# Moving two samples' cached values from TensorE to VectorE and ScalarE in a hybrid decoder layer

## The chip, the core and the metric

One core of one Trainium2 chip runs the whole layer as one program. The metric is device time in microseconds (us); lower is better. Time before: median 2462.08 us of 3 runs (2461.53 to 2462.41).

## What is computed

One layer of a decoder for a prompt of 512 positions and 8 samples of one token each, 520 columns in all, D_MODEL 2048. A pre-norm and one input projection give q, k, v for 8 stick-breaking attention heads of 128 and u, v for 8 channel groups of a gated MLP. Both outputs are normalised and go through one output projection, then follow a SwiGLU FFN (5632 wide) and an input-embedding gate. The samples attend to 1024 cached positions each, read through a page table: 8 pages of 128 positions. What the change touches is the last line for the samples:

```python
k_past = cache_k[i][page_table]   # (8 samples, 1024, 8 heads, 128), v_past alike
after = lax.cumsum(log_keep, axis=3, reverse=True) - log_keep
a = jnp.where(causal, jnp.exp(jax.nn.log_sigmoid(z) + after), 0.0)
return jnp.einsum('bhqk,bkhd->bqhd', a, v)      # sum over keys of weight x value
```

All is float32; projections are made of three float32r products (high x high, low x high, high x low).

## The kernel before

Activations lie feature-major: 128 partitions of features by 520 columns. The mixer is a sequence of 56 units (`u`), each one weight unit of 16 blocks of 128x128, six products of 260 columns per block. Units 0 to 7 make q, 8 to 23 the MLP's halves, 24 to 39 (from U_KV = 24) k and v in turn, 40 to 47 (U_OUT) the output projection's half fed by the MLP (o_cm), 48 to 55 (U_OUT_SB) its half fed by attention. From unit 40 a unit makes two output tiles, T_OUT + 0 to 31. After unit 55 come the FFN and the gate.

Every engine runs its own list in program order, and waits on semaphores:

- **TensorE** (lines 2067 to 2129) makes the blocks of unit u. Small products are slotted ahead of a block through `between`: in odd units from 25 `sum_later` at block 2, `sum_head` at 6, `attend` at 12, and `scores` after the unit; in even units a transposition at 8. `weigh_values` (line 2036) does a page of cached values: 8 products with a 128x128 stationary block of values and one moving column of weights, put at blocks 7, 11 and 14. Eight pages of a sample take three units from V_FIRST[b] on; samples 6 and 7 (counted from 0) are at units 34 to 36 and 38 to 40. A page's sums lie in spare columns of the unit's PSUM tile. Before a tile, TensorE waits until the tile two back is read (`out_read`, line 1944).
- **VectorE** (line 1500 on) starts its unit u when unit u-1 has ended: `take_values(u-1)`, the take of the tile (`take`, or `out_tile` from u = 41: take times cm_r or sb_r, then add into h), `low_w(u+1)`, then in even units to 38 `keep_head` (which waits for `soft_done`), in odd ones `exponents`, `mask_weights`, `normalise`. `low_x` (line 1359) makes a low part of x. From unit 40 a second `out_tile(2*(u-40))` ends the unit; tiles 0, 6 and 12 first wait for h_in.
- **ScalarE** (line 1020 on) makes w_hi of unit u+1 (`split_w`, when unit u-1 has ended), the logits, exponentials and roots, copies attention out of PSUM, and splits x_hi.
- **POOL** (line 759 on) works through jobs sorted by a due time written as a unit number: page loads into three slots (v_ring's two, acc), each waiting for the page three before to be used; squares of each MLP group and each attention head (512 columns) summed into cm_r and sb_r; and at last, after the last `v_read`, the squares of the 8 sample columns of each head into sb_r, 16 small operations (lines 823 to 826), which signal `sb_sum_done`.
- **SP** (line 655 on) issues loads and stores in the order of its loop over u. Two of h's loads matter here:

```python
                if u == U_OUT + 4:

                    sp.wait_ge(av_ready, HEADS)
                    sp.wait_ge(sb_sum_done, 1)
                    sp.dma_start(h[:, H_PAGES:KT, :], x_t[:, H_PAGES:KT, :]).then_inc(h_in[2], 16)
```

This one (tiles 12 to 15) is line 689; line 684 loads tiles 6 to 11. At the head of its turn u, SP issues the weight load of unit u+3, once unit u+1's low part is done. The sum of sb_r over partitions, its root (ScalarE) and its reciprocal (VectorE) are made in unit SB_ROOT = 45, and x's attention half is split into high and low in units 45, 46 and 47 (3, 3 and 2 heads).

Of the kernel before, what the change touches and what calls it, by code (L numbers as in the profile page):

```python
# [203 lines left out]
CONSTS = 11  # L204
RING = 2
CM_ROOT = U_OUT - 2
SB_ROOT = U_OUT + 5

SB_SPLITS = {U_OUT_SB - 3 + i: range(3 * i, min(3 * i + 3, HEADS)) for i in range(3)}
K_PERIOD = 10  # L210
K_WIDE = K_PER[0] * (U_KV - K_PERIOD)
N_PAGES = SAMPLES * PAGES
# [9 lines left out]


SUM_END = [p + 1 + (p + 1) % 2 for p in LAST_K]
V_FIRST = [16, 19, 22, 25, 28, 31, 34, 38]
V_SLOTS = 3


def v_unit(j):

    b, pg = divmod(j, PAGES)
    return V_FIRST[b] + pg // 3


def v_pages(u):

    return [j for j in range(SAMPLES * PAGES) if v_unit(j) == u]


V_UNITS = [u for u in range(V_FIRST[0], V_FIRST[-1] + 3) if v_pages(u)]  # L240


DIAG = lambda kb: slice(kb * P, (kb + 1) * P)
# [24 lines left out]
def build(nc, w_units, x_t, p_t, cache_k, cache_v, page_table, g_mix, g_out, g_ffn, g_ple, g_q, g_k,  # L268
# [6 lines left out]
    with ExitStack() as ctx:  # L275
# [136 lines left out]

        def v_slot(j):

            return acc[:, :] if j % V_SLOTS == RING else v_ring[:, j % V_SLOTS, :]

        def o_s_ps(u):

            return out_ps[:, 2 * ((tiles_before(u + 1) - 1) % 2) + 1, HALF:HALF + HEADS]

        def raw_slot(slot):

# [63 lines left out]
        consts_in = sem("consts_in")  # L486
        table_in = sem("table_in")
        k_in = [sem(f"k_in{i}") for i in range(3)]
        v_in = [sem(f"v_in{i}") for i in range(V_SLOTS)]
        q_rows_out = sem("q_rows_out")  # L490
        q_rows_in = sem("q_rows_in")
        h_in = [sem(f"h_in{i}") for i in range(3)]
# [71 lines left out]
        ones_built = sem("ones_built")  # L564
        pool_step = sem("pool_step")
        v_used = sem("v_used")
        v_read = sem("v_read")
        h_sum_done = sem("h_sum_done")
        cm_sum_done = sem("cm_sum_done")
# [34 lines left out]
        def _(sp):  # L604
# [50 lines left out]
            for u in range(U_FFN):  # L655
                if u < U_FFN - 1:
                    load_unit(u + 3)
                if u == K_PERIOD - 1:

                    sp.wait_ge(pair_read, 1)  # L660
                    sp.dma_start(q_rows_dram, acc[0:SAMPLES, :]).then_inc(q_rows_out, 16)
                    sp.wait_ge(q_rows_out, 16)

                while u >= K_PERIOD - 1 and next_k < N_PAGES and \
                        (k_before(next_k) is None or k_period(k_before(next_k)) <= u):
                    load_k(next_k)
                    next_k += 1
                if U_KV + 2 <= u <= U_OUT and u % 2 == 0:
                    i = (u - U_KV - 2) // 2
                    sp.wait_ge(norm_done, 2 * HEADS + i + 1)  # L670
                    sp.dma_start(k_t[i], k_head[:, :]).then_inc(k_out, 16)
                    sp.wait_ge(out_read, U_KV + 2 * i + 2)
                    sp.dma_start(v_t[i], y[:, 1, :]).then_inc(v_out, 16)
                if u == U_KV + 2:
                    sp.wait_ge(cm_done, HEADS)
                    sp.dma_start(chunk_v_t, chunk_v[:, :, :]).then_inc(chunk_out, 16)
                if u == LAST_K[-1] + 3:

                    sp.wait_ge(z_s_done, SAMPLES)
                    sp.dma_start(h[:, 0:H_KEYS, :], x_t[:, 0:H_KEYS, :]).then_inc(h_in[0], 16)  # L680
                if u == V_UNITS[-1] + 2:

                    sp.wait_ge(v_used, N_PAGES)
                    sp.dma_start(h[:, H_KEYS:H_PAGES, :], x_t[:, H_KEYS:H_PAGES, :]).then_inc(h_in[1], 16)
                if u == U_OUT + 4:

# [72 lines left out]
        def _(pool):  # L759
# [25 lines left out]

            def load_v(j):
                page = pool.value_load(table[0:1, j:j + 1], min_val=0, max_val=N_PHYS - 1)
                if j >= V_SLOTS:
                    pool.wait_ge(v_used, j - V_SLOTS + 1)
                elif j % V_SLOTS == RING:  # L790
                    pool.wait_ge(q_rows_out, 16)
                pool.dma_start(v_slot(j),
                               cache_v[bass.ds(page, 1), :, :].rearrange("a p n -> (a p) n"))\
                    .then_inc(v_in[j % V_SLOTS], 16)

            def add_squares(x, total, cols, done=pool_step):
                chained(pool.tensor_tensor(pool_sq[:, cols], x, x, ALU.mult))
# [5 lines left out]
                    pool.wait_ge(done, 1)  # L803


            jobs = [(v_unit(j - V_SLOTS) + 0.8, "load", j) for j in range(V_SLOTS, N_PAGES)]
            jobs += [(U_MLP + 3.5 + 2 * i, "mlp", i) for i in range(HEADS)]
            jobs += [(U_KV + 3.7 + 2 * i, "attention", i) for i in range(HEADS)]
            pool.wait_ge(table_in, 16)
            pool.wait_ge(x_lo_done, KT)  # L810
            pool.wait_ge(sq_done, X_SQUARES)
# [73 lines left out]
        def _(act):  # L885
# [76 lines left out]
            def weights_of_sample(u):  # L962

                if u - 1 in SUM_END:
# [3 lines left out]
                        act.wait_ge(v_used, PAGES * (b - 2))  # L968
                    act.activation(a_s[:, b % 3, :], z_s[:, :], ACT.Exp).then_inc(a_s_done, 1)

            def sample_job(u):

                if u not in SUM_END:
                    return []
                act.wait_ge(z_s_done, SUM_END.index(u) + 1)
                return [(soft_s[:, :], z_s[:, :], soft_s_done)]
# [43 lines left out]
            for u in range(1, U_FFN):  # L1020
# [35 lines left out]
                elif u < U_OUT and u % 2 == 1:  # L1056
# [8 lines left out]
                    rstd(2 * HEADS + i)  # L1065
                    if not i:
                        weights_of_sample(u)
                    if i:
                        take_attention(i - 1)
                elif u <= U_OUT:  # L1070
# [38 lines left out]
                if u == SB_ROOT:  # L1109
                    root(2, HEADS * P, sb_r[:, :])  # L1110
                    load_ln_exp()
                if u in SB_SPLITS:
                    for k in SB_SPLITS[u]:
                        split(x_hi[:, k, :], q[:, k, :], gain_out[:, k:k + 1])
# [226 lines left out]
        def _(dve):  # L1341
# [72 lines left out]

            def take_values(u):

                if u not in V_UNITS:
                    return
                b = v_pages(u)[0] // PAGES
                dve.wait_ge(out_done, tiles_before(u + 1))  # L1420
                sums = q[:, :, PROMPT + b]
                if u == V_FIRST[b]:
                    dve.tensor_copy(sums, o_s_ps(u)).then_inc(v_read, 1)
                else:
                    dve.wait_ge(v_read, V_UNITS.index(u))
                    dve.tensor_tensor(sums, sums, o_s_ps(u), ALU.add).then_inc(v_read, 1)

            def weigh_sample(b):
                dve.wait_ge(later_s_ready, b + 1)
# [70 lines left out]
            for u in range(1, U_FFN):  # L1500
# [63 lines left out]
                elif u <= U_OUT and u % 2 == 0:  # L1564
# [5 lines left out]
                    low_w(u + 1, 1)  # L1570
                    score_next()
                    if u < U_OUT:
                        keep_head(i)
                    if u in SUM_END:
                        keep_sample(SUM_END.index(u))
# [9 lines left out]
                if U_KV < u < U_OUT and u % 2 == 1:  # L1585
# [10 lines left out]
                    if i:  # L1596
                        dve.wait_ge(k_out, 16 * i)
                    normalise(2 * HEADS + i, k_head[:, :], y[:, t % 2, :], gain_k[:, 0:1])
                if u == CM_ROOT:
                    invert(1, cm_r[:, :])  # L1600
                if u == SB_ROOT:
                    invert(2, sb_r[:, :])
# [4 lines left out]
                    keep_sample(SUM_END.index(u))  # L1607
                while pages:
                    score_next()
                if u == U_OUT_SB + 2:  # L1610
                    for k in range(2):
                        dve.wait_ge(p_hi_done, k + 1)
                        dve.tensor_tensor(p_lo[:, k, :], p_raw[:, k, :], p_hi[:, k, :], ALU.subtract)\
                            .then_inc(p_lo_done, 1)
# [303 lines left out]
        def _(pe):  # L1918
# [117 lines left out]
            def weigh_values(j, u):  # L2036
# [5 lines left out]
                pe.wait_ge(v_in[j % V_SLOTS], 16 * (j // V_SLOTS + 1))  # L2042
                if j == pages[0] and V_UNITS.index(u) > 1:
                    pe.wait_ge(v_read, V_UNITS.index(u) - 1)
                for hd in range(HEADS):
                    at = pg * HEADS + hd
                    mm = pe.matmul(o_s_ps(u)[:, hd:hd + 1], v_slot(j)[:, hd * P:(hd + 1) * P],  # L2047
                                   a_s[:, b % 3, at:at + 1], start=False, stop=j == pages[-1],
                                   skip_group_check=True)
                mm.then_inc(v_used, 1)  # L2050

            def sum_later_sample(b, u):
                pe.wait_ge(keep_s_done, b + 1)
# [13 lines left out]
            for u in range(1, U_FFN):  # L2067
# [30 lines left out]

                for at, j in zip((14, 11, 7), reversed(v_pages(u))):
                    between[at] = lambda j=j, u=u: weigh_values(j, u)  # L2100
                if u - 1 in SUM_END:
                    between[4] = lambda u=u: sum_later_sample(SUM_END.index(u - 1), u - 1)

# [286 lines left out]
```

## Time and profile before

| | us |
|---|---|
| median of 3 runs | 2462.08 |
| profiled execution | 2461.91 |
| its span | 2460.3 |
| TensorE busy in the span | 2428.4 |
| VectorE busy | 1724.0 |
| ScalarE busy | 1118.4 |
| POOL busy | 374.2 |

The granted TensorE clock was 0.999 of 2.4 GHz. The mixer's units 34 to 48 lie from 566.7 to 794 us; stretches are named by the time at which VectorE begins its turn, which is when TensorE has ended the projection of the unit before. A row of a stretch is: its ends, its length, busy us (x instructions) of TensorE, its weight loads, VectorE, ScalarE and POOL, then the granted clock, the DMA engines' busy share and GB/s. A row in order of time is: start us, duration us, engine, line, operation. "x2" behind an entry means that two instructions are merged in it; a bracket gives the idle time of the engine before it and what ended that.

### The profile page before, as it was taken

The page shows a single profiled execution, that of the slowest core. Times are in us where ns is not written, and L with a number is a line of the kernel's source. Part 1 is how long each engine was busy: PE and PEld are TensorE (multiplying, and loading weights), DVE is VectorE, ACT ScalarE, POOL GpSimd, SP SyncE. Part 2 cuts the span into 40 slices and gives each one's busy share as a digit, 9 for nine tenths or more (in the row PEclk, how much of TensorE's full clock was granted, in tenths as well). Part 3 has the DMA queues.
Part 4 walks back from the last instruction along what each step waited for, and adds up shares of the span by engine and source line. Part 5 has one row for each costly group of instructions (what it writes and reads, how often), then busy time and mean ns, then how long its engine had stood idle before and what let it go on. Part 6 is the DMA issues. An engine that isn't in the chain of part 4 may idle for free.

```text
span 2460.3 us, 47595 instructions
## 1 busy us (share of the span) xinstructions
PE 2428.4 (99%) x19952; PEld 2405.6 (98%) x19952; DVE 1724.0 (70%) x2172; ACT 1118.4 (45%) x1655; POOL 374.2 (15%) x375
## 2 busy tenths in 40 slices
PE   8999999999999998999999999999999999999999
PEld 7999999999999998999999999999999999999999
DVE  5379767564446478888888888888888888877333
ACT  6333233333433365555555555555555555555221
POOL 0011111111001220121212121111112121223000
PEclk9999999999999999999999999999999999999999
DMA  6256766463423452474757565656566666695323
GB/s 217 94 189 213 249 224 220 164 209 124 160 104 105 146 173 90 123 175 125 169 130 164 134 160 137 163 136 159 141 152 146 148 152 144 155 197 215 122 86 104
DMA packets 135590, 382.61 MB, mean 156 GB/s; under 512 B 14026, under 2 KB 58186, under 8 KB 126674
## 3 DMA queue, kind: packets, MB, share of 16 engines
q1 hardware_dynamic: 72450, 285.16, 33.9%
q0 software_dynamic: 62640, 94.28, 20.2%
q8 instruction: 158, 2.59, 0.4%
q14 instruction: 54, 0.44, 0.1%
q10 hardware_dynamic: 288, 0.14, 0.0%
HBM read 309.18 MB, written 73.55 MB: 156 GB/s over the span
## 4 chain that ended last, share of the span: by engine, by line
PE 86%; DVE 9%; ACT 2%; issue 2%; DMA 1%; SPq 0%; ACTq 0%; DVEq 0%; POOL 0%
PE out_ps L1925 24%; PE tok_mix L2158 15%; PE pair_ps L2158 12%; PE out_ps L2142 9%; PE out_ps L2158 8%; PE out_ps L2047 4%; PE out_ps L2231 4%; PE pair_ps L2231 2%; DVE w_sum L1637 2%; DVE w_lo L1625 2%; PE pair_ps L1964 1%; PE tok_mix L2231 1%; DVE w_lo L1630 1%; ACT w_hi L1134 1%; DVE staging L1786 1%
## 5 line engine op out<-in xcount | busy, mean ns | idle before, releaser
L1925 PE MATMUL out_ps<-x_hi,w_hi 128*128 128x260 f32 x1792 | 378.6, 292 | 10.1 <-DVE w_lo L1480 8.3
L1134 ACT ACTIVATE w_hi<-w_sum 128x1024 fp32r<-128x1024 f32 (+1 forms) x252 | 215.4, 855 | 343.1 <-DVE w_sum L1637 247.9
L1925 PE MATMUL out_ps<-x_hi,w_lo 128*128 128x260 f32 x1792 | 361.1, 283 | 0.0
L1925 PE MATMUL out_ps<-x_lo,w_hi 128*128 128x260 f32 x1792 | 360.8, 283 | 0.0
L1625 DVE TENSOR_TENSOR w_lo<-w_sum,w_hi 128x1024 fp32r<-128x1024 f32 (+1 forms) x252 | 244.7, 971 | 135.0 <-ACT w_hi L1134 134.5
L1134 ACT ACTIVATE w_hi<-w_raw 128x1024 fp32r<-128x1024 f32 (+1 forms) x306 | 261.2, 865 | 133.7 <-PE out_ps L2142 102.4
L2158 PE MATMUL tok_mix<-op_hi,w_hi 128*128 128x260 f32 x1056 | 297.3, 282 | 2.1 <-ACT part L1176 1.9
L2158 PE MATMUL tok_mix<-op_hi,w_lo 128*128 128x260 f32 x1056 | 298.1, 282 | 0.0
L2158 PE MATMUL tok_mix<-op_lo,w_hi 128*128 128x260 f32 x1056 | 297.5, 282 | 0.0
L1925 PEld LDWEIGHTS out_ps<-x_hi,w_hi 128*128 128x128 f32 x1792 | 278.5, 189 | 12.7 <-DVE w_lo L1480 8.3
L854 POOL DMA_DIRECT2D h_dram<-staging x110 | 146.9, 1489 | 926.7 <-DVE staging L1786 909.4
L1925 PEld LDWEIGHTS out_ps<-x_hi,w_lo 128*128 128x128 f32 x1792 | 276.5, 189 | 0.0
L1925 PEld LDWEIGHTS out_ps<-x_lo,w_hi 128*128 128x128 f32 x1792 | 276.5, 189 | 0.0
L2158 PE MATMUL pair_ps<-op_hi,w_hi 128*128 128x260 f32 x880 | 248.5, 282 | 9.1 <-DVE op_lo L1828 5.0
L2158 PE MATMUL pair_ps<-op_hi,w_lo 128*128 128x260 f32 x880 | 248.9, 283 | 0.0
L2158 PE MATMUL pair_ps<-op_lo,w_hi 128*128 128x260 f32 x880 | 248.5, 282 | 0.0
L1625 DVE TENSOR_TENSOR w_lo<-w_raw,w_hi 128x1024 fp32r<-128x1024 f32 x172 | 209.5, 1222 | 44.7 <-ACT w_hi L1134 44.7
L898 ACT ACTIVATE w_hi<-w_raw 128x1024 fp32r<-128x1024 f32 x114 | 114.3, 1050 | 210.8 <-PE out_ps L1925 210.6
L2158 PEld LDWEIGHTS tok_mix<-op_hi,w_hi 128*128 128x128 f32 x1056 | 198.2, 188 | 2.6 <-ACT part L1176 2.1
L2158 PEld LDWEIGHTS tok_mix<-op_hi,w_lo 128*128 128x128 f32 x1056 | 198.5, 188 | 0.0
L2158 PEld LDWEIGHTS tok_mix<-op_lo,w_hi 128*128 128x128 f32 x1056 | 198.2, 188 | 0.0
L2158 PEld LDWEIGHTS pair_ps<-op_hi,w_hi 128*128 128x128 f32 x880 | 165.8, 188 | 10.0 <-issue 8.3
(291 smaller groups left out, 6106.3 us busy)
## 6 DMA issues: line engine op xcount, KB each, us to landing
w_raw<-w_units SPq DMA_DIRECT2D x239, 512.0 KB, 4.1
w_raw<-w_units SPq DMA_DIRECT2D x57, 1024.0 KB, 5.0
w_fifth<-w_units SPq DMA_DIRECT2D x58, 512.0 KB, 3.8
h_dram<-staging POOLq DMA_DIRECT2D x110, 260.0 KB, 7.0
k_ring<-cache_k SPq DMA_DIRECT2D x50, 512.0 KB, 5.2
v_ring<-cache_v POOLq DMA_DIRECT2D x43, 512.0 KB, 4.7
h_dram<-part POOLq DMA_DIRECT2D x50, 260.0 KB, 6.6
acc<-cache_v POOLq DMA_DIRECT2D x21, 512.0 KB, 5.2
```

Of the source, the lines that this page charges most:

```text
L854: pool.dma_start(dst, stage(k), accum_op=op).then_inc(h_added[DOWN_SLOT[k]], 16)
L898: act.activation(w_hi[:, u % 2, cols], w_raw[:, u % 2, cols], ACT.Copy).then_inc(hi_done, 1)
L1134: act.activation(dst, src, ACT.Copy).then_inc(hi_done, 1)
L1625: dve.tensor_tensor(slot(w_lo, job), src, slot(w_hi, job), ALU.subtract).then_inc(lo_done, 1)
L1630: dve.tensor_tensor(as_blocks(slot(w_lo, job)), src, as_blocks(slot(w_hi, job)), ALU.subtract)\
L1637: dve.tensor_tensor(dst, x, w, op).then_inc(w_summed, 1)
L1786: dve.tensor_tensor(stage(k), stage(k), (bank_y, bank_v)[n], ALU.add).then_inc(sums_staged, 1)
L1925: mm = pe.matmul(out_ps[:, 2 * (t % 2) + a, 0:HALF], w[:, u % 2, cols], x[:, a * HALF:(a + 1) * HALF], start=first and n == 0, stop=last a ...
L2047: mm = pe.matmul(o_s_ps(u)[:, hd:hd + 1], v_slot(j)[:, hd * P:(hd + 1) * P], a_s[:, b % 3, at:at + 1], start=False, stop=j == pages[-1], s ...
L2142: mm = pe.matmul(tile[:, a, :], w, x[:, a * HALF:(a + 1) * HALF], start=first and n == 0, stop=last and n == 2)
L2158: mm = pe.matmul(acc, w, x[:, g, :], start=fresh and g == 0 and n == 0, stop=g == GROUPS - 1 and n == 2, skip_group_check=True)
L2231: mm = pe.matmul(DOWN_BANKS[i][:, a, :], w, x, start=fresh and c == 0 and n == 0, stop=c == 1 and n == 2, skip_group_check=True)
```

## The change

Samples 0 to 5 stay as they are. Sample 6 (pages 48 to 55): VectorE multiplies each page in place by its weights, broadcast along the 128 values of a head, and adds the pages to one total, two pages a unit in units 35 to 38. Sample 7 (pages 56 to 63): ScalarE scales each head's 128 columns of a page by its weight, 8 instructions a page, in units 39 and 41 to 44; VectorE adds the pages in units 40 and 42 to 45. A total is summed over partitions by TensorE with 8 products against one column of ones (`sum_total`), at block 14 of units 39 and 45. Four more slots for pages and a total are cut out of o_cm, once its low parts are made. SB_ROOT moves from unit 45 to 47, the splits of attention to units 46 and 47 (5 and 3 heads), cm_r's reciprocal from unit 38 to 39, POOL's job for the last head to 43.9, and h's load of tiles 6 to 11 from SP's turn 42 to 40. SP's load at turn 44 keeps its place and its waits. V_UNITS becomes a list of pairs (unit, sample) and ends with 45, so that the last `v_read` comes at the start of VectorE's turn 46.

```diff
 CM_ROOT = U_OUT - 2
-SB_ROOT = U_OUT + 5
-
-SB_SPLITS = {U_OUT_SB - 3 + i: range(3 * i, min(3 * i + 3, HEADS)) for i in range(3)}
+SB_ROOT = U_OUT + 7
+
+SB_SPLITS = {U_OUT_SB - 2: range(0, 5), U_OUT_SB - 1: range(5, HEADS)}
...
-V_FIRST = [16, 19, 22, 25, 28, 31, 34, 38]
+V_FIRST = [16, 19, 22, 25, 28, 31]
 V_SLOTS = 3
+O_SLOTS = 4
+BY_TENSOR = len(V_FIRST)
+N_TENSOR = BY_TENSOR * PAGES
+SIXTH, SEVENTH = N_TENSOR, N_TENSOR + PAGES
+
+
+WEIGH_UNIT = dict(zip(range(SIXTH, N_PAGES), (35, 35, 36, 36, 37, 37, 38, 38) + (39, 39, 41, 41, 42, 43, 43, 44)))
+ADD_UNIT = dict(zip(range(SIXTH, N_PAGES), (35, 35, 36, 36, 37, 37, 38, 38) + (40, 40, 42, 42, 43, 44, 44, 45)))
+V_REDUCE = {39: BY_TENSOR, 45: BY_TENSOR + 1}
+V_SLOT = [j % V_SLOTS for j in range(SIXTH + 1)] + [1 + n % 2 for n in range(PAGES - 1)] + [2, 1, 4, 5, 6, 4, 5, 6]
+V_TOTAL = {BY_TENSOR: V_SLOT[SIXTH], BY_TENSOR + 1: V_SLOTS}
...
+def v_freed(j):
+
+    return v_unit(j) if j < N_TENSOR else ADD_UNIT[j]
...
+def v_before(j):
+
+    return max((i for i in range(j) if V_SLOT[i] == V_SLOT[j]), default=None)
...
+        def v_place(i):
+
+            if i >= V_SLOTS:
+                first = (i - V_SLOTS) * HEADS * P
+                return o_cm[:, :, :].rearrange("p h n -> p (h n)")[:, first:first + HEADS * P]
+            return acc[:, :] if i == RING else v_ring[:, i, :]
...
@@ block.sync
-                if u == V_UNITS[-1] + 2:
-
-                    sp.wait_ge(v_used, N_PAGES)
+                if u == U_OUT:
+
+                    sp.wait_ge(v_used, N_TENSOR)
+                    sp.wait_ge(total_used, 1)
+                    sp.wait_ge(v_added, added(SEVENTH + 1))
                     sp.dma_start(h[:, H_KEYS:H_PAGES, :], x_t[:, H_KEYS:H_PAGES, :]).then_inc(h_in[1], 16)
                 if u == U_OUT + 4:
 
...
@@ block.gpsimd
-                if j >= V_SLOTS:
-                    pool.wait_ge(v_used, j - V_SLOTS + 1)
-                elif j % V_SLOTS == RING:
+                before = v_before(j)
+                if before is None and V_SLOT[j] >= V_SLOTS:
+                    pool.wait_ge(x_lo_done, KT + HEADS)
+                elif before is not None and before < N_TENSOR:
+                    pool.wait_ge(v_used, before + 1)
+                elif before is not None:
+                    pool.wait_ge(v_added, added(before))
+                elif V_SLOT[j] == RING:
                     pool.wait_ge(q_rows_out, 16)
...
-            jobs = [(v_unit(j - V_SLOTS) + 0.8, "load", j) for j in range(V_SLOTS, N_PAGES)]
+            freed = [U_OUT - 0.3 if v_before(j) is None else v_freed(v_before(j)) for j in range(V_SLOTS, N_PAGES)]
+            jobs = [(freed[j - V_SLOTS] + 0.8, "load", j) for j in range(V_SLOTS, N_PAGES)]
             jobs += [(U_MLP + 3.5 + 2 * i, "mlp", i) for i in range(HEADS)]
-            jobs += [(U_KV + 3.7 + 2 * i, "attention", i) for i in range(HEADS)]
+            jobs += [(U_KV + 3.7 + 2 * i, "attention", i) for i in range(HEADS - 1)]
+            jobs += [(U_OUT + 3.9, "attention", HEADS - 1)]
...
@@ block.scalar
+            def weigh_page(j):
+
+                b, pg = divmod(j, PAGES)
+                act.wait_ge(a_s_done, b + 1)
+                act.wait_ge(v_in[V_SLOT[j]], 16 * (v_turn(j) + 1))
+                for hd in range(HEADS):
+                    values = v_slot(j)[:, hd * P:(hd + 1) * P]
+                    at = pg * HEADS + hd
+                    ins = act.activation(values, values, ACT.Copy, scale=a_s[:, b % 3, at:at + 1])
+                ins.then_inc(v_scaled, 1)
...
                     if not i:
                         weights_of_sample(u)
+                    weigh_pages(u)
                     if i:
                         take_attention(i - 1)
...
                     take_attention(HEADS - 1)
+                if u > U_OUT:
+                    weigh_pages(u)
...
+                if u == min(SB_SPLITS):
+                    act.wait_ge(v_read, len(V_UNITS))
                 if u in SB_SPLITS:
...
@@ block.vector
+            def weigh_page(j):
+
+                b, pg = divmod(j, PAGES)
+                dve.wait_ge(v_in[V_SLOT[j]], 16 * (v_turn(j) + 1))
+                values = v_slot(j).rearrange("p (h d) -> p h d", h=HEADS)
+                weights = a_s[:, b % 3, pg * HEADS:(pg + 1) * HEADS].unsqueeze(2).to_broadcast([P, HEADS, P])
+                if pg == 0:
+                    dve.wait_ge(a_s_done, b + 1)
+                chained(dve.tensor_tensor(values, values, weights, ALU.mult), v_weighed)
+
+            def add_page(j):
+
+                b, pg = divmod(j, PAGES)
+                if b > BY_TENSOR:
+                    dve.wait_ge(v_scaled, pg + 1)
+                if j == SEVENTH + 1:
+                    dve.wait_ge(x_lo_done, KT + HEADS)
+                total = v_place(V_TOTAL[b])
+                chained(dve.tensor_tensor(total, v_slot(j - 1) if pg == 1 else total, v_slot(j), ALU.add), v_added)
+
+            def pages_of(u):
+
+                for j in range(SIXTH, N_PAGES):
+                    if j < SEVENTH and WEIGH_UNIT[j] == u:
+                        weigh_page(j)
+                    if ADD_UNIT[j] == u and j % PAGES:
+                        add_page(j)
...
                     score_next()
                     if u < U_OUT:
+                        pages_of(u)
                         keep_head(i)
...
-                if u == CM_ROOT:
+                if u == CM_ROOT + 1:
                     invert(1, cm_r[:, :])
...
                 while pages:
                     score_next()
+                if u % 2 or u >= U_OUT:
+                    pages_of(u)
...
@@ block.tensor
+            def sum_total(u, b):
+
+                pe.wait_ge(v_added, added(PAGES * b + PAGES - 1))
+                pe.wait_ge(v_read, V_UNITS.index((u, b)))
+                total = v_place(V_TOTAL[b])
+                for hd in range(HEADS):
+                    mm = pe.matmul(o_s_ps(u, b)[:, hd:hd + 1], total[:, hd * P:(hd + 1) * P], ones[:, 0:1],
+                                   start=False, stop=True, skip_group_check=True)
+                mm.then_inc(total_used, 1)
...
                 for at, j in zip((14, 11, 7), reversed(v_pages(u))):
                     between[at] = lambda j=j, u=u: weigh_values(j, u)
+                if u in V_REDUCE:
+                    between[14] = lambda u=u: sum_total(u, V_REDUCE[u])
```

## Rows read from the trace of the kernel before

**Rows 1.** The page: the span, and the first line of its busy times.

```profile
span 2460.3 us, 47595 instructions
...
PE 2428.4 (99%) x19952; PEld 2405.6 (98%) x19952; DVE 1724.0 (70%) x2172; ACT 1118.4 (45%) x1655; POOL 374.2 (15%) x375
```

**Rows 2.** The chain of waits, unit 36: start us, us, what.

```profile
617.98 2.15 PE out_ps L1925 x18
620.13 1.68 PE out_ps L2047 x16
621.81 2.27 PE out_ps L1925 x18
```

**Rows 3.** Stretches: units 37 to 39, 42, 43, 45 (columns: see above).

```profile
627.40:645.90 18.50, 18.50 (x139) 17.06 (x138) 6.61 (x10) 5.88 (x8) 2.17 (x2) 1.00 0.47 172
645.90:666.30 20.40, 20.40 (x169) 19.97 (x168) 11.05 (x11) 11.40 (x12) 1.80 (x4) 1.00 0.42 131
666.30:689.60 23.30, 23.30 (x182) 21.86 (x181) 6.20 (x8) 5.72 (x8) 2.71 (x3) 1.00 0.21 68
...
718.80:736.00 17.20, 17.20 (x130) 15.89 (x129) 7.41 (x9) 3.28 (x3) 0.00 (x0) 1.00 0.40 155
736.00:747.50 11.50, 11.50 (x98) 11.50 (x97) 6.03 (x6) 2.49 (x3) 6.72 (x18) 1.00 0.28 93
...
759.10:771.50 12.40, 12.40 (x103) 12.28 (x102) 10.58 (x10) 7.24 (x8) 0.00 (x0) 1.00 0.26 86
```

**Rows 4.** VectorE's groups by form, 560 to 830 us: key product.

```profile
L1385 DVE TENSOR_TENSOR k_ring<-k_ring,q_rows 128x1024 f32<-128x1024 f32 x2 | 2.4, 1223 | 0.0
```

**Rows 5.** VectorE in order of time, unit 38.

```profile
647.07 2.36 DVE L1354 TENSOR_TENSOR w_lo<-w_raw,w_hi 128x1024 fp32r<-128x1024 f32 x2 [0.42 <-ACT w_hi L898]
653.71 1.49 DVE L1444 SCALAR_TENSOR_TENSOR keep<-z,soft 128x1280 f32<-128x1280 f32 x1 [4.27 <-ACT soft L960]
```

**Rows 6.** POOL in order of time, units 35 and 37; v_ring's landings.

```profile
609.26 0.59 POOL L792 DMA_DIRECT2D v_ring<-cache_v  x1 [1.22 <-issue]
...
644.77 1.28 POOL L798 TENSOR_TENSOR sb_r<-sb_r,pool_sq 128x512 f32<-128x512 f32 x1
...
DMA to landing us min/median/max: 3.4/3.7/5.1
```

**Rows 7.** ScalarE: two forms (busy us, mean ns), one instruction of unit 39.

```profile
L946 ACT ACTIVATE v_tok<-tok_mix 128x512 f32<-128x512 f32 x14 | 8.3, 596 | 39.5 <-PE tok_mix L1976 39.5
...
L969 ACT ACTIVATE a_s<-z_s 128x64 f32<-128x64 f32 x8 | 2.0, 251 | 16.9 <-DVE dot_pad L1434 16.9
...
684.92 0.60 ACT L951 ACTIVATE q<-tok_mix 128x512 f32<-128x512 f32 x1 [8.69 <-PE tok_mix L2032]
```

**Rows 8.** POOL, then VectorE, in order of time, unit 43.

```profile
739.73 2.15 POOL L798 TENSOR_TENSOR sb_r<-sb_r,pool_sq 128x512 f32<-128x512 f32 x1
741.96 0.20 POOL L797 TENSOR_TENSOR pool_sq<-q 128x8 f32<-128x8 f32 x1
...
742.80 0.54 POOL L798 TENSOR_TENSOR sb_r<-sb_r,pool_sq 128x8 f32<-128x8 f32 x1
...
746.47 0.20 POOL L798 TENSOR_TENSOR sb_r<-sb_r,pool_sq 128x8 f32<-128x8 f32 x1
...
737.52 3.21 DVE L1354 TENSOR_TENSOR w_lo<-w_raw,w_hi 128x1024 fp32r<-128x1024 f32 x2
...
742.55 0.72 DVE L1471 TENSOR_TENSOR h<-h,sq 128x520 f32<-128x520 f32 x1
```

**Rows 9.** VectorE in order of time, unit 45.

```profile
763.15 3.40 DVE L1368 RECIPROCAL sb_r<-sb_r 128x520 f32<-128x520 f32 x1 [0.20 <-ACT sb_r L914]
766.59 2.10 DVE L1363 SCALAR_TENSOR_TENSOR x_lo<-q,gain_out,x_hi 128x520 fp32r<-128x520 f32 x3
```

**Rows 10.** Line 689, h's tiles 12 to 15 (1040 KB): landing.

```profile
DMA to landing us min/median/max: 6.7/6.7/6.7
```

**Rows 11.** Line 610, weights of 1024 KB, 560 to 830 us: landing.

```profile
DMA to landing us min/median/max: 4.6/5.0/8.4
```

More of the change, by code:

```diff
@@ L224, with v_pages, v_turn, added @@
 SUM_END = [p + 1 + (p + 1) % 2 for p in LAST_K]
-V_FIRST = [16, 19, 22, 25, 28, 31, 34, 38]
+V_FIRST = [16, 19, 22, 25, 28, 31]
 V_SLOTS = 3
-def v_unit(j):
+O_SLOTS = 4
[7 more added lines that the diff above has]
+V_TOTAL = {BY_TENSOR: V_SLOT[SIXTH], BY_TENSOR + 1: V_SLOTS}
+def v_unit(j):
+    return V_FIRST[j // PAGES] + j % PAGES // 3
+def v_pages(u):
+    return [j for j in range(N_TENSOR) if v_unit(j) == u]
+def v_freed(j):
+    return v_unit(j) if j < N_TENSOR else ADD_UNIT[j]
+def v_turn(j):
+    return V_SLOT[:j].count(V_SLOT[j])
+def v_before(j):
+    return max((i for i in range(j) if V_SLOT[i] == V_SLOT[j]), default=None)
+def added(j):
     b, pg = divmod(j, PAGES)
[L232 to L240, printed above, removed]
+    return (PAGES - 1) * (b - BY_TENSOR) + pg
+V_UNITS = sorted([(u, b) for b in range(BY_TENSOR) for u in range(V_FIRST[b], V_FIRST[b] + 3)] + list(V_REDUCE.items()))
 DIAG = lambda kb: slice(kb * P, (kb + 1) * P)
@@ L413, in v_slot, with o_s_ps @@
         def v_slot(j):
-            return acc[:, :] if j % V_SLOTS == RING else v_ring[:, j % V_SLOTS, :]
-        def o_s_ps(u):
-            return out_ps[:, 2 * ((tiles_before(u + 1) - 1) % 2) + 1, HALF:HALF + HEADS]
+            return v_place(V_SLOT[j])
+        def v_place(i):
[3 more added lines that the diff above has]
+            return acc[:, :] if i == RING else v_ring[:, i, :]
+        def o_s_ps(u, b):
+            first = HALF + HEADS * (b % 2)
+            return out_ps[:, 2 * ((tiles_before(u + 1) - 1) % 2) + 1, first:first + HEADS]
         def raw_slot(slot):
@@ L488, in build @@
         k_in = [sem(f"k_in{i}") for i in range(3)]
-        v_in = [sem(f"v_in{i}") for i in range(V_SLOTS)]
+        v_in = [sem(f"v_in{i}") for i in range(V_SLOTS + O_SLOTS)]
         q_rows_out = sem("q_rows_out")
@@ L566, in build @@
         v_used = sem("v_used")
+        v_weighed = sem("v_weighed")
+        v_added = sem("v_added")
+        total_used = sem("total_used")
+        v_scaled = sem("v_scaled")
         v_read = sem("v_read")
@@ L793, in load_v @@
                                cache_v[bass.ds(page, 1), :, :].rearrange("a p n -> (a p) n"))\
-                    .then_inc(v_in[j % V_SLOTS], 16)
+                    .then_inc(v_in[V_SLOT[j]], 16)
             def add_squares(x, total, cols, done=pool_step):
@@ L969, in weights_of_sample, with weigh_pages @@
                     act.activation(a_s[:, b % 3, :], z_s[:, :], ACT.Exp).then_inc(a_s_done, 1)
+            def weigh_page(j):
[7 more added lines that the diff above has]
+                ins.then_inc(v_scaled, 1)
+            def weigh_pages(u):
+                for j in range(SEVENTH, N_PAGES):
+                    if WEIGH_UNIT[j] == u:
+                        weigh_page(j)
             def sample_job(u):
@@ L1415, in take_values @@
             def take_values(u):
[L1417 to L1426, printed above, removed]
+                for n, (v_u, b) in enumerate(V_UNITS):
+                    if v_u == u:
+                        dve.wait_ge(out_done, tiles_before(u + 1))
+                        sums = q[:, :, PROMPT + b]
+                        if b >= BY_TENSOR or u == V_FIRST[b]:
+                            dve.tensor_copy(sums, o_s_ps(u, b)).then_inc(v_read, 1)
+                        else:
+                            dve.wait_ge(v_read, n)
+                            dve.tensor_tensor(sums, sums, o_s_ps(u, b), ALU.add).then_inc(v_read, 1)
+            def weigh_page(j):
[17 more added lines that the diff above has]
+                    if j < SEVENTH and WEIGH_UNIT[j] == u:
+                        weigh_page(j)
+                    if ADD_UNIT[j] == u and j % PAGES:
+                        add_page(j)
             def weigh_sample(b):
@@ L2041, in weigh_values @@
                     pe.wait_ge(a_s_done, b + 1)
-                pe.wait_ge(v_in[j % V_SLOTS], 16 * (j // V_SLOTS + 1))
-                if j == pages[0] and V_UNITS.index(u) > 1:
-                    pe.wait_ge(v_read, V_UNITS.index(u) - 1)
+                pe.wait_ge(v_in[V_SLOT[j]], 16 * (v_turn(j) + 1))
+                n = V_UNITS.index((u, b))
+                if j == pages[0] and n > 1:
+                    pe.wait_ge(v_read, n - 1)
                 for hd in range(HEADS):
                     at = pg * HEADS + hd
-                    mm = pe.matmul(o_s_ps(u)[:, hd:hd + 1], v_slot(j)[:, hd * P:(hd + 1) * P],
+                    mm = pe.matmul(o_s_ps(u, b)[:, hd:hd + 1], v_slot(j)[:, hd * P:(hd + 1) * P],
                                    a_s[:, b % 3, at:at + 1], start=False, stop=j == pages[-1],
```

## The prediction

> **What bounds the kernel now.** I read the page first: of a span of 2460.3 us TensorE is busy 2428.4, and every other engine far less [rows 1]. So any work that leaves TensorE shortens the run, as long as nothing makes TensorE wait instead. The profiled execution took 2461.91 us (1.6 around its span), 0.17 below the median of the three runs, 2462.08; I make the sum against 2461.91 and add the 0.17 back. A measurement of this kernel can tell about 0.2%, 4.9 us, from no change.
>
> Second, the chain of work through the mixer. It is all TensorE, without a gap, and says what a page of values costs there: a piece of 1.68 us for its 8 products (two records each) [rows 2]. The 18 records of projection behind a page take 2.27 us where the 18 ahead of it take 2.15, so the page also costs 0.12 at its seam. I take 1.79 (other seams show 0.11); bounds are 1.68 and, for seams at both ends, 1.85.
>
> Third, the stretches by unit [rows 3]. In units 38 and 39 TensorE is busy throughout, VectorE 11.05 of 20.4 us and 6.20 of 23.3, ScalarE 11.40 and 5.72. There is room for the moved work by its sum. What must be checked is its place in each queue.
>
> **TensorE's part.** Sixteen pages leave, at units 34, 35, 36 and 38, 39, 40; two totals of 8 products against a column of ones come, at 39 and 45. They have the form of a page, so I price them as one. Net 14 x 1.79 = 25.1 us saved (bounds 23.5 and 25.9). It comes off fully if nothing below is late.
>
> **VectorE in units 35 to 38.** It gets 8 products and 7 sums of 128x1024. The nearest row is the key product of the same shape, 1.22 us [rows 4]; with its wait 1.25. Even units put four of them, 5.0 us, between low_w and keep_head. In unit 38 (start 645.9) low_w ends 3.5 us in, and keep_head, which waits for ScalarE's soft, starts 7.8 us in [rows 5]. So 4.3 us were idle and page work fills them. One gate is ahead: pages 54 and 55 are loaded by POOL behind its squares of head 5, which end at 646.05, 0.1 us into the unit; the load follows 1.2 us later [rows 6] and lands in 3.7 us (at most 5.1), 5 to 6.5 us into the unit. Then four operations end at 10.3, and keep_head with its 4.8 us at about 15. The unit itself shrinks from 20.4 to 20.4 - 5.4 = 15.0. Behind the waiting instruction stand keep_head and the next take; TensorE needs keep_head two blocks (1.35 us) into unit 39, at 16.3. Slack 1.3 us: cost zero, and up to 1.5 if the page lands late or goes unhidden. Unit 36 is alike. Its sample bookkeeping stands behind keep_head and is wanted only at block 4. In odd units the page work stands last, where VectorE has done its 6.20 us of 23.3 [rows 3] and waits for the next take. The same holds for the inversion of cm_r, moved from unit 38 to 39: 3.40 us by its twin [rows 9], beside TensorE's work.
>
> **ScalarE.** It gets 64 scalings of 128x128. Bounds are 0.25 us (the 128x64 exponential) and 0.60 (128x512); by the line between them about 0.3 [rows 7]. In unit 39 two pages are 16 of them, some 5 us, where ScalarE had 8.69 us idle ahead of taking the attention, from 10 us into the unit [rows 7]; with two pages gone ahead of it the attention comes 15 us in, so 5 fit. In units 41 to 44 ScalarE is busy 2.5 to 3.3 us of 11.5 to 17.2 [rows 3] and gets at most 5. Cost nothing; uncovered, at 0.6 each, 5 us late, and later units still hide that, because VectorE adds a unit later (the last page: scaled in 44, added in 45, used at block 14 of 45).
>
> **VectorE, units 40 to 45.** Seven sums, at most two a unit (2.5 us), in units like 42 and 43, where it is busy 7.41 of 17.2 and 6.03 of 11.5 [rows 3]. Hidden: its next take of a first half comes no earlier than 5.8 us in, and TensorE needs that only at the next unit's start.
>
> **What moves late: the sb sum.** This is the part with a price. POOL squares the eight samples' columns, 16 small operations, only after the last v_read. That read was at unit 41; it is now at the start of unit 46 (call this T). Three things wait for the result. The sum over partitions, moved to unit 47, is not late. But SP's load of x into h, tiles 12 to 15, still stands at its old place in the loop, unit 44, and waits for sb_sum_done; behind it in SP's queue stands the weight load of unit 48. And VectorE waits for that h in out_tile(12), in unit 46.
>
> POOL's 16 operations took from 741.96 to 746.67, 4.7 us [rows 8]. There VectorE was mostly idle. Where it was not, they blocked each other: POOL's sum at 742.80 took 0.54 in place of 0.20 beside VectorE's h sum (742.55, 0.72), POOL's 128x512 sum took 2.15 beside low_w, and the two low_w 3.21 in place of 2.36. In unit 46 POOL starts with VectorE's busiest stretch: one h sum (0.70), two low_w (2.36) and five x_lo (0.70 each, from 2.10 for three [rows 9]), all reading two SBUF tensors, 6.5 us together. With every one of the eight holding POOL once, less POOL's gap of 0.08 each: 0.3 + 4.7 + 6.5 - 0.6 = 10.8 us after T. Bounds: 5.0 (no hold) and 11.4.
>
> The Trainium skill ("SBUF — State Buffer", section Who interferes with whom) says that a VectorE instruction with two SBUF inputs and a GpSimd one that reads SBUF fully block each other, the first to issue holding the port; by that rule the sum is ready near 10.8, without it near 5.0. The trace agrees, with the 0.54 and the 2.15 above.
>
> Then SP issues (0.1), the load lands in 6.7 us (its own row [rows 10]; at least 5 by a weight load of the same size [rows 11]), and the take adds 0.75: T + 18.3. TensorE reaches the end of unit 46 at T + 11.5 [rows 3] and its next tile needs exactly that take. **Wait: 6.8 us**; bounds 0 (5.0 + 0.1 + 5.0 + 0.75 = 10.9, before 11.5) and about 8.5.
>
> Next in line is unit 48. Its weights, issued at T + 11.3 behind the h load, land in at most 8.4 us (T + 19.7) [rows 11]; ScalarE splits them, then root and reciprocal (3.40), three x_lo and the take of tile 14 follow, which I put at T + 30.2, against TensorE's T + 18.3 + 12.4 [rows 3] = 30.7. Nothing, or up to 2 us.
>
> SP's other h load moves from 42 to 40 and waits for page 57's sum, some 10 us into unit 40; the weight load ahead of it is out by then and the next is due in unit 41, so nothing queues up. It and the page loads share DMA engines that the rows show 0.21 to 0.47 busy [rows 3].
>
> **Sum.** -25.1 + 6.8 = -18.3; 2461.91 - 18.3 + 0.17 = 2443.8 us. Past unit 56 all is gated by TensorE's own progress and carries the shift unchanged.
>
> **Rivals.**
> 1. *POOL is not held up, or the load is quick* (0.22). For: small operations may slip in between VectorE's. Against: the 0.54 row. Wait 0 to 2: 2437 to 2439.
> 2. *Forecast* (0.58): wait 4 to 8.5, 2441 to 2446.
> 3. *More than one place is late* (0.12): keep_head misses unit 39 by 1.5, the take of tile 14 misses unit 48 by 2, page scalings hold split_w once by 2: 2443.8 + 5.5, so 2447 to 2456. For: slacks of 1.3 and 0.4 us. Against: all rest on measured rows.
> 4. *Slower* (0.05), one mechanism: VectorE stands at v_in ahead of keep_head in units 36 and 38, because POOL loads those pages behind its squares. Each us beyond the slack of 1.3 is a us of TensorE, twice. To lose 18.3 and a measurable 5 more, each load must be 13 us late, landing in 17 us where the rows show 3.7, at most 5.1: about 2467.
> The remaining 0.03 is for gains and losses that meet within 0.2%. That the change doesn't do what it says I exclude: pages 48 to 63 leave TensorE by the loop's own bound.
>
> **Range.** 2436.5 (first rival, full saving) to 2448.5: it takes in rival 1, the forecast and the start of 3. Faster by over 0.2%: 0.92; within 0.2%: 0.03; slower: 0.05.
>
> **What would show it.** TensorE's page products down from 1024 records to 768, plus 32 for totals; units 35, 36, 38 at 18.0, 14.1, 15.0 us. One wait of TensorE near the start of unit 47, on VectorE's take, of about 7 us, itself behind DMA of h. POOL's 16 small operations stretched to some 10 us. If TensorE waits in 39, rival 3 or 4; if nowhere, rival 1 and 25 us saved. I am wrong if the saving per page is not near 1.8, or if the wait stands elsewhere.

## The result, and the profile after

The changed kernel took 2445.25 us (median of 4 runs, 2443.67 to 2446.13) against 2462.24 for the kernel before on the same chip: a ratio of 0.993, 95% interval 0.9913 to 0.9948. The forecast was 2443.8. (One of e_wfirst's four executions below took 6080.08 us; its median is of the other three.) The profiled execution's span went from 2460.3 to 2443.6 us, 16.7 less. The number is close; two of its terms were off in opposite directions, and a third was missing, as the rows below show.

The page of the changed kernel, with the first lines of its busy times and of its chain (compare rows 1):

```profile
span 2443.6 us, 47247 instructions
...
PE 2409.5 (99%) x19728; PEld 2386.2 (98%) x19728; DVE 1749.0 (72%) x2190; ACT 1137.6 (47%) x1719; POOL 377.9 (15%) x375
...
PE 84%; DVE 9%; ACT 2%; issue 2%; DMA 1%; POOL 0%; SPq 0%; ACTq 0%; DVEq 0%; POOLq 0%
```

TensorE has 224 records less (112 products of two) and VectorE 25.0 us more work. TensorE's share of the chain went from 86% to 84%. The stretches of the changed kernel, for units 36, 38, 39, 45, 46, 47 and 48 (columns as in rows 3):

```profile
599.00:613.10 14.10, 14.10 (x116) 13.78 (x115) 13.14 (x17) 8.75 (x11) 1.85 (x4) 1.00 0.69 225
...
631.60:646.60 15.00, 15.00 (x120) 14.57 (x120) 9.33 (x8) 11.38 (x11) 2.43 (x5) 1.00 0.66 211
646.60:668.70 22.10, 20.11 (x150) 18.46 (x150) 12.74 (x14) 10.53 (x23) 2.30 (x2) 1.00 0.22 73
...
734.70:747.90 13.20, 13.20 (x114) 13.20 (x113) 6.30 (x7) 2.01 (x2) 0.00 (x0) 1.00 0.00 1
747.90:763.20 15.30, 12.11 (x99) 11.94 (x98) 8.56 (x12) 5.11 (x7) 7.51 (x16) 0.94 0.34 128
763.20:777.90 14.70, 14.70 (x102) 14.30 (x101) 10.61 (x11) 7.24 (x8) 0.00 (x0) 0.83 0.41 155
777.90:789.50 11.60, 11.60 (x99) 11.60 (x98) 5.16 (x6) 2.01 (x2) 0.00 (x0) 1.00 0.39 138
```

Unit 38 went from 20.4 us [rows 3] to 15.0 and unit 36 measures 14.1, both as forecast. Unit 35 measures 16.9, not the forecast 18.0: VectorE, busy until then, began its turn at 582.2, 1.2 us after ScalarE, which waits for the same end of unit 34. Units 34 and 35 together went from 43.0 to 32.3, which is six pages of 1.79. Unit 39 should have taken 23.3 - 3 x 1.79 + 1.79 = 19.7 and took 22.1, with TensorE busy 20.11. Unit 46 took 15.3 in place of 11.5, busy 12.11. Unit 47 took 14.7 in place of 12.4 with TensorE busy throughout, but its granted clock was 0.83, and 0.94 in the stretch before. So three things were paid: about 2.3, 3.7 and 2.4 us. 25.1 - 2.3 - 3.7 - 2.4 = 16.7, the whole difference of the spans.

For TensorE itself the last two divide otherwise, because the bound between units 46 and 47 is VectorE's turn, at 763.27, and TensorE had gone on at 762.65. TensorE stood 3.2 us. Its granted clock fell to half (1.2 GHz) at about 761.5, while it still stood, and rose again at 768.3; these are its first 5.65 us of work behind the wait:

```profile
762.65:768.30 5.65, 5.65 (x22) 5.25 (x23) 4.35 (x5) 3.98 (x5) 0.00 (x0) 0.50 0.60 254
```

So the low clock cost 5.65 / 2 = 2.8 us, and wait and clock together 6.0 of the 6.1.

TensorE's waits, changed kernel, whose longest is over 1.9 us (engine, line, for whom: us in total, times, longest). The first two belong to the start and to the FFN and are about as they were; the third is in unit 47, the fourth in 39:

```profile
PE out_ps L2029 <- DVE w_lo L1581: 7.8, 1, 7.8
PE pair_ps L2275 <- DVE op_lo L1932: 5.0, 1, 5.0
PE out_ps L2029 <- DVE sq L1452: 3.2, 1, 3.2
PE pair_ps L2113 <- DVE soft L1553: 2.0, 1, 2.0
```

**The wait in unit 39.** The chain of waits of the changed kernel through unit 38, pieces left out:

```profile
628.75 0.61 ACT q L1003
...
629.44 1.05 POOL pool_sq L847
...
630.55 1.30 POOL sb_r L848
...
634.22 8.40 DMA v_ring<-cache_v
...
642.71 1.24 DVE v_ring L1509
643.97 1.23 DVE v_ring L1519
645.23 1.50 DVE keep L1545
...
650.01 1.13 PE pair_ps L2113 x2
```

It is the gate that the prediction named: POOL's squares of head 5, then the load of page 55, then VectorE's product and sum, then keep_head, then TensorE's sum_later in unit 39. But the load of page 55 took 8.4 us, where rows 6 show 3.7 and at most 5.1. It was also issued 1.2 us behind that of page 54, which landed in 4.9. VectorE in order of time, unit 38, shows both page waits (compare rows 5, where keep_head starts 7.8 us into the unit; here it is 13.6):

```profile
637.97 1.23 DVE L1509 TENSOR_TENSOR acc<-acc,a_s 128x1024 f32<-128x1024 f32 x1 [2.75 <-DMA acc<-cache_v]
639.23 1.23 DVE L1519 TENSOR_TENSOR v_ring<-v_ring,acc 128x1024 f32<-128x1024 f32 x1
642.71 1.23 DVE L1509 TENSOR_TENSOR v_ring<-v_ring,a_s 128x1024 f32<-128x1024 f32 x1 [2.26 <-DMA v_ring<-cache_v]
```

The product with a broadcast operand costs 1.23 us, as its nearest row did (rows 4: 1.22). ScalarE's 16 scalings of two pages took 4.79 us in units 41 and 43, 0.30 each, as estimated.

**The wait in unit 47.** POOL in order of time, changed kernel, unit 46 (compare rows 8), then VectorE there:

```profile
748.35 0.20 POOL L847 TENSOR_TENSOR pool_sq<-q 128x8 f32<-128x8 f32 x1 [27.77 <-DVE q L1496]
748.64 0.21 POOL L848 TENSOR_TENSOR sb_r<-sb_r,pool_sq 128x8 f32<-128x8 f32 x1
748.92 0.69 POOL L847 TENSOR_TENSOR pool_sq<-q 128x8 f32<-128x8 f32 x1
749.69 1.18 POOL L848 TENSOR_TENSOR sb_r<-sb_r,pool_sq 128x8 f32<-128x8 f32 x1
750.95 1.06 POOL L847 TENSOR_TENSOR pool_sq<-q 128x8 f32<-128x8 f32 x1
752.08 0.59 POOL L848 TENSOR_TENSOR sb_r<-sb_r,pool_sq 128x8 f32<-128x8 f32 x1
...
756.84 0.20 POOL L848 TENSOR_TENSOR sb_r<-sb_r,pool_sq 128x8 f32<-128x8 f32 x1
```

```profile
749.58 2.37 DVE L1428 TENSOR_TENSOR w_lo<-w_raw,w_hi 128x1024 fp32r<-128x1024 f32 x2
751.87 3.43 DVE L1437 SCALAR_TENSOR_TENSOR x_lo<-q,gain_out,x_hi 128x520 fp32r<-128x520 f32 x5
761.80 0.70 DVE L1452 TENSOR_TENSOR sq<-out_ps,cm_r 128x520 f32<-128x520 f32 x1 [6.50 <-DMA h<-x_t]
```

Eight of POOL's sixteen operations are stretched: 0.69, 1.18, 1.06 and five of 0.59. The chain of sixteen lasts 8.7 us, from 748.35 to 757.04, where it was 4.7. SP issues the h load at 757.12 and it lands in 4.7; VectorE's take, 6.5 us idle before it, starts at 761.80, and TensorE goes on at 762.65, having stood 3.19 us.

### The profile page after: what moved, and what is told of

The parts are those of the page before. It is cut to its first block, busy times and chain, and to the rows that moved or that the text cites. A ratio compares the mean times of both kernels' runs of the same rounds, so it can differ in the third digit from the quotient of the medians.

```text
span 2443.6 us, 47247 instructions
## 1 busy us (share of the span) xinstructions
PE 2409.5 (99%) x19728; PEld 2386.2 (98%) x19728; DVE 1749.0 (72%) x2190; ACT 1137.6 (47%) x1719; POOL 377.9 (15%) x375
## 4 chain that ended last, share of the span: by engine, by line
PE 84%; DVE 9%; ACT 2%; issue 2%; DMA 1%; POOL 0%; SPq 0%; ACTq 0%; DVEq 0%; POOLq 0%
PE out_ps L2029 24%; PE tok_mix L2275 15%; PE pair_ps L2275 12%; PE out_ps L2259 9%; PE out_ps L2275 8%; PE out_ps L2348 5%; PE out_ps L2152 3%; PE pair_ps L2348 3%; DVE w_lo L1729 2%; DVE w_sum L1741 2%; PE tok_mix L2348 1%; PE pair_ps L2068 1%; ACT w_hi L1208 1%; DVE w_lo L1734 1%; DMA w_raw<-w_units 1%
```

## The experiments

Each time is a median; the kernel before took 2461.67 beside the first four and 2462.01 beside the last three. The 95% interval of each ratio reaches 0.17%, some 4 us, to either side. So the times alone do not settle differences of 0.5 to 2.5 us between two versions; there the traces carry the argument.

**Only the products leave TensorE (e_price).** An edit of the kernel before, which leaves out seven of the eight heads' sums for samples 6 and 7:

```diff
-                for hd in range(HEADS):
+                for hd in range(HEADS if j < 6 * PAGES else 1):
                     at = pg * HEADS + hd
```

> The kernel before, with 112 products left out and nothing put in their place: of the 16 pages of samples 6 and 7, TensorE makes only the first head's product of the eight (the other heads' sums for these two samples are left out). That is the same net number of products that the change takes from TensorE. Theory (a page costs 1.79 us at every place, and 14 pages' worth are worth 25.1): 2462.1 - 25.1 = 2437.0, no waits of TensorE in units 34 to 48, no lower clock there. Rival (products beside projections are partly hidden, so they are worth less, and the change lost nothing but some of this saving): 2443 to 2446.

Measured: 2436.86 us, ratio 0.9899 (0.9882 to 0.9915), 24.8 us less than the kernel before beside it; TensorE waits nowhere from unit 34 to 48 (busy 240.00 of the 240 us from 560 to 800), and its clock is whole until the FFN. The products are worth 1.77 to 1.79 us a page in full, so the change loses some 8 us elsewhere.

**POOL's order (e_due).** On the changed kernel:

```diff
-            jobs += [(U_KV + 3.7 + 2 * i, "attention", i) for i in range(HEADS - 1)]
+            jobs += [(U_KV + 3.9 + 2 * i, "attention", i) for i in range(HEADS - 1)]
```

> The changed kernel, with POOL's squares of heads 0 to 6 due 0.2 of a unit later, so that they stand behind the page loads of the same unit instead of ahead. Theory (the 2.0 us wait of TensorE in unit 39 comes from pages 54 and 55 landing late, ahead of keep_head in VectorE's queue): both pages land before VectorE comes to them in unit 38, keep_head starts about 8.5 us into the unit instead of 13.5, the wait in unit 39 is gone: 2445.2 - 2.2 = 2443.0; the wait at unit 47 stays. Rival (VectorE simply has too much ahead of keep_head in unit 38, wherever the pages are): the wait stays at 1 to 2 us, 2445.

Measured: 2443.22 us, ratio 0.9921 (0.9904 to 0.9937), 2.0 less than the changed kernel. VectorE in order of time, e_due, unit 38 (start 632.3):

```profile
635.95 1.21 DVE L1509 TENSOR_TENSOR acc<-acc,a_s 128x1024 f32<-128x1024 f32 x1
...
640.98 1.49 DVE L1545 SCALAR_TENSOR_TENSOR keep<-z,soft 128x1280 f32<-128x1280 f32 x1
```

No wait for a page is left, keep_head starts 8.6 us into the unit, and TensorE's wait in unit 39 is gone: the unit takes 19.8 us in place of 22.1. So it was the page's lateness, not the amount of VectorE's work. The wait at unit 47 stays, at 3.3. The low clock behind it is shorter here, about 3.5 us in place of 6.8.

**The h load freed from the sample squares (e_scratch).** On the changed kernel (`squared` is a new semaphore):

```diff
-                    sp.wait_ge(sb_sum_done, 1)
+                    sp.wait_ge(squared, 1)
...
-                    add_squares(q[:, i, 0:PROMPT], sb_r, slice(0, PROMPT))
+                    add_squares(q[:, i, 0:PROMPT], sb_r, slice(0, PROMPT), squared if i == HEADS - 1 else pool_step)
...
-                            sb_sum_done if i == HEADS - 1 else pool_step)
+                            sb_sum_done if i == HEADS - 1 else pool_step, z)
```

> The changed kernel, with the sample squares put in a buffer that h does not cover (the free z), so that SP's load of h, tiles 12 to 15, waits only for the last head's squares in unit 43. Theory (that load is what TensorE waits for at the start of unit 47, and the half-clock stretch of 6.8 us behind it follows from that wait): the wait of 3.2 us and the half-clock stretch are both gone, unit 46 back to 11.5 us and unit 47 to 12.4: 2445.2 - 3.7 - 2.4 = 2439.1. Rival A (sample squares still bound unit 47 through the sum of sb_r): a wait of 1 to 3 us moves into unit 47 or 48. Rival B (the lower clock has nothing to do with the wait): it stays somewhere in units 46 to 48, 2441.5.

Measured: 2439.59 us, ratio 0.9909 (0.9892 to 0.9925), 5.7 less than the changed kernel. The stretches of e_scratch, units 46 and 47:

```profile
748.40:759.95 11.55, 11.55 (x98) 11.55 (x97) 8.51 (x12) 5.11 (x7) 8.00 (x16) 1.00 0.26 92
759.95:772.30 12.35, 12.35 (x102) 12.23 (x101) 10.57 (x10) 7.24 (x8) 0.00 (x0) 1.00 0.23 86
```

Both units are back at 11.55 and 12.35 us, at a whole clock, though POOL's sixteen operations are as slow as before (8.00 us busy). POOL's lateness alone cost nothing; it cost through h's load. The wait in unit 39 is still there, 2.4 us in this trace.

**SP's order (e_wfirst).** On the changed kernel:

```diff
-                if u == U_OUT + 4:
+                if u == U_OUT + 6:
 
                     sp.wait_ge(av_ready, HEADS)
```

> The changed kernel, with SP's load of h, tiles 12 to 15, and its waits moved from turn 44 of SP's loop to turn 46, so that the weight loads of units 48 and 49 stand ahead of it. Theory (the h load alone counts, and it cannot start before the sample squares are summed): nothing changes but ScalarE's wait of 11 us for unit 48's weights, the wait at unit 47 stays at 3 to 4 us: 2445 within 0.7. Rival (the weight load held back in SP's queue counts too): 2 us or more are won.

Measured: 2444.75 us, ratio 0.993 (0.991 to 0.9949): no gain clear of noise, 0.5 less than the changed kernel. ScalarE no longer waits 11 us for unit 48's weights. TensorE's wait is 3.3, and the low clock stands behind it again, for 6.8 us as in the changed kernel. What SP held back behind its wait was not needed sooner.

**Both repairs (e_both).** The edits of e_due and e_scratch together.

> The changed kernel with both repairs: POOL's squares of heads 0 to 6 due behind the page loads (as in e_due), and the sample squares in z, so that h's load waits only for the last head's squares (as in e_scratch). Theory (the two waits are independent and all that was lost besides the clock): all 25.1 us of the removed products come through, no wait of TensorE over 1 us from unit 34 to unit 48 and no half-clock stretch there: 2462.0 - 25.1 = 2437.0. Rival (one repair uncovers something that the other hid, such as VectorE late at unit 48): 2439 or more.

Measured: 2437.98 us (2437.10 to 2438.96), ratio 0.9902 (0.9886 to 0.9919), 24.0 less than the kernel before beside it and 7.3 less than the changed kernel. In e_both TensorE waits nowhere between units 34 and 48:

```profile
560.00:800.00 240.00, 240.00 (x1909) 232.53 (x1908) 157.60 (x182) 112.38 (x174) 34.80 (x45) 1.00 0.41 140
```

It is the best version of the study, and within 1.1 us of e_price, where the products were simply left out.

**VectorE's x_lo out of POOL's way (e_xlo_late).** On the changed kernel:

```diff
-                if u in SB_SPLITS:
+                if u in SB_SPLITS and u > min(SB_SPLITS):
...
                     out_tile(2 * (u - U_OUT), cm_r if u < U_OUT_SB else sb_r)
+                if u == min(SB_SPLITS):
+                    for k in SB_SPLITS[u]:
+                        low_x(k, q[:, k, :], gain_out[:, k:k + 1])
```

> The changed kernel, with VectorE's five x_lo of unit 46 moved from ahead of out_tile(12) to behind it. Theory (POOL's small squares are held up by VectorE's operations with two SBUF inputs, one each): five of POOL's sixteen take 0.20 again in place of 0.59, the chain of sixteen shrinks from 8.7 to 6.8 us, h lands 1.9 us earlier, TensorE's wait at unit 47 falls from 3.2 to 1.3, and the half-clock stretch may go with it: 2443.3, or 2441 without that stretch. Rival (POOL is slow there for another reason, such as its own start or ScalarE's splits, which stay): the chain stays at 8.7 us, 2445.

Measured: 2443.80 us, ratio 0.9924 (0.9908 to 0.9941). POOL in order of time, e_xlo_late, unit 46:

```profile
751.46 1.06 POOL L847 TENSOR_TENSOR pool_sq<-q 128x8 f32<-128x8 f32 x1
752.60 0.20 POOL L848 TENSOR_TENSOR sb_r<-sb_r,pool_sq 128x8 f32<-128x8 f32 x1
...
755.38 0.20 POOL L848 TENSOR_TENSOR sb_r<-sb_r,pool_sq 128x8 f32<-128x8 f32 x1
```

The three operations beside the h sum and low_w stay slow (0.69, 1.18, 1.06); the five that ran beside x_lo take 0.20. The chain is 6.7 us (748.87 to 755.58), and TensorE's wait for the take 1.3. So x_lo, a VectorE operation with two inputs in SBUF, is what held those five; for the h sum and low_w the overlap in time says the same, but they were not moved. The total fell by 1.45 us, less than the wait, though the clock is whole here from 758 to 780 us. The x_lo now make VectorE late in unit 47, and TensorE stands a second time, for 1.3 us. From the start of unit 46 to the second take of unit 48 this trace is 2.9 us shorter than the changed kernel's, so the other 0.9 of its span's 2.0 less was lost again outside these units.

**A wait made by VectorE alone (e_filler).** On e_both:

```diff
+                if u == min(SB_SPLITS):
+                    for _ in range(2):
+                        chained(dve.reciprocal(soft[:, 0:TOK], soft[:, 0:TOK]))
                 if u >= U_OUT:
```

> The kernel e_both with two reciprocals of 128x520 (3.4 us each, on the spare tile soft) put on VectorE ahead of out_tile(12) in unit 46, so that TensorE must wait again at the start of unit 47, this time for no DMA and no POOL. VectorE's x_lo end 7.2 us into unit 46, the take then at 14.1 to 14.8, so the wait is about 3.2 us. Theory (the half-clock stretch follows from TensorE's own idling): a stretch at half clock of 3.4 to 6.8 us stands right behind the wait and costs 1.2 to 2.4 us over it: 2437.0 + 3.2 + 1.2 to 2.4, so 2441.4 to 2442.6. Rival (it came with the late DMA or POOL work): the clock stays whole, 2440.2.

Measured: 2442.25 us (2440.83 to 2443.02), 4.3 over e_both. The profiled execution is the quickest, 2440.83. In it TensorE waits 3.5 us, and the stretch behind the wait (unit 47, with most of that wait in it) has a whole clock:

```profile
757.90:773.00 15.10, 12.12 (x98) 12.03 (x98) 13.99 (x13) 6.85 (x8) 0.00 (x0) 1.00 0.21 71
```

So here the wait was not enough to lower the clock. The other three executions took 1.0 to 2.2 us more, with mean clocks of 0.997, 0.996 and 0.998, which leaves room for such a stretch in some of them; no trace shows where. The expectation is not met in the one place where it was looked for.

That TensorE's idling by VectorE alone can be followed by the low clock is shown elsewhere in the traces, the one before the change included. In the FFN of the kernel before, TensorE stands 4.96 us for VectorE's op_lo with POOL and the DMA engines idle for the first 4.5 us of it, and goes on at 927.31:

```profile
PE pair_ps L2158 <- DVE op_lo L1828: 5.0, 1, 5.0
...
927.31:930.10 2.79, 2.79 (x13) 2.79 (x14) 2.79 (x3) 0.68 (x1) 0.00 (x0) 0.50 0.43 163
```

In e_filler the same wait is followed by 3.1 us at 0.50, and a wait of 2.3 us for VectorE's w_lo, with the DMA engines idle, by 3 us more. So the rival, that the low clock belongs to a late DMA or to POOL's work, falls; that it follows every such wait falls too.

## Why the prediction was right

- **TensorE's part: right.** 14 pages x 1.79 = 25.1. Units 36 and 38 came out at 14.1 and 15.0 as forecast, e_price took off 24.8 and e_both 24.0.
- **VectorE in 35 to 38: the price right, the zero wrong.** Its operations cost what the key product did. The step that failed is "lands in 3.7 us (at most 5.1)": page 55 took 8.4, keep_head ended at 649.95 where TensorE wanted it at about 648.0, and TensorE stood 2.0 us, 2.3 over the unit. The prediction also gave pages 54 and 55 one landing, where the second load was issued 1.2 us behind the first. I had taken the landing from page loads of the kernel before, issued at other points of the unit. That page 55 shared the DMA engines with unit 41's weights and the k and v stores, issued 1.0 to 2.3 us behind it, fits the stretch's DMA share of 0.66 against 0.42 [rows 3], but was not tried apart. (Two weight loads issued right behind h's load, at 757.49, left that one at 4.7.) e_due shows that the order of the load against POOL's squares decides. The prediction gave this as a possible 1.5 us, and as part of its third rival.
- **ScalarE, and VectorE from 40 to 45: right.** No wait of TensorE stands there.
- **The sb sum: right in place and in mechanism, too dear.** Forecast a wait of 6.8 us, measured 3.2. Two terms were mis-sized. POOL was done 9.1 us after T, not 10.8: I added POOL's own 0.20 to each time that it was blocked, but a blocked operation took 0.59 beside an x_lo that repeats every 0.68, so its last part ran beside VectorE's next; and VectorE was not slowed (2.37 for two low_w, 2.36 before), unlike beside POOL's wide operations [rows 8]. And h landed in 4.7, not 6.7: in the kernel before, a weight load was issued 0.1 us ahead of it; here none was. In e_scratch, where one is again issued right ahead, h's load lands in 7.1, and in e_due, e_wfirst and e_xlo_late, without one, in 4.8. With these, 9.1 + 0.1 + 4.7 + 0.8 - 11.5 = 3.2, as measured. Two bounds of the prediction do not come out of its rows: "at least 5" for the landing (rows 11 show 4.6), and "about 8.5" for the wait, where 11.4 + 0.1 + 6.7 + 0.75 - 11.5 makes 7.5. Rival 1 was half right: POOL was held up, and e_xlo_late shows by what for five of eight, but the load was quick. The wait of 3.2 lies between rival 1's 0 to 2 and the forecast's 4 to 8.5, in neither.
- **Unit 48's start: right.** The held weight load cost nothing, and e_wfirst shows it.
- **Missing: the clock.** The prediction had no term for it. 5.65 us of TensorE's work behind the wait ran at 1.2 GHz, which cost 2.8 us.

The three errors are -3.6, +2.3 and +2.8 us. They sum to 1.5, against 1.45 between forecast and median. So the closeness of the total is luck in good part: more than one place was late, as the third rival says, but with a total inside the forecast's 2441 to 2446. The sign is no luck, since all that was lost, 8.4 us, is a third of what the products gave.

## What to carry to other kernels

When work leaves the bounding engine, its gain is the products' own price, and what is lost is found by asking of every wait that the moved work now feeds, who else stands behind it: here a DMA into memory that a 16-operation scratch happened to share. Take a transfer's landing time from rows with the same neighbours in the queue and on the DMA engines; here 3.7 became 8.4 where other loads and stores were issued close behind (not tried apart), and 6.7 became 4.7 without a load right ahead. A load that gates a busy engine belongs ahead of the same queue's side work: changing a due time by 0.2 took 2.3 us off unit 39.

## What the runs showed of the hardware that I had not expected

POOL's small operations were lengthened by VectorE's two-input ones (0.20 to 0.59, and up to 1.18) with no cost to VectorE that shows (two low_w in 2.37 for 2.36), while POOL's 128x512 operations had slowed VectorE too (two low_w in 3.21 for 2.36). The rule of the Trainium skill ("SBUF — State Buffer", section Who interferes with whom), that whichever comes second fully blocks, fits POOL's side; of VectorE's side this case shows only that an 8-column POOL operation does not block it measurably.

A stretch at the lower TensorE clock, in the profiled run of the changed kernel, began within a wait of 3.2 us, went on behind it and cost 2.8 us. Waits of 3.3 us at the same place in e_due and e_wfirst had one too, of about 3.5 and 6.8 us. The changed kernel's wait of 2.0 us in unit 39 was followed by a whole clock, and so was e_filler's of 3.5 us; e_filler's of 2.3 us in the FFN was not. So such a wait can be followed by the lower clock and need not be, and its length alone does not decide; what does stays open.
